# Second-half expert weights requested by the activation engine instead of the sync engine in a two-layer mixture-of-experts kernel

## The reference

```python
# 32 experts; every token goes to 2 of them
h = jax.nn.silu(xi @ w1[e]) * (xi @ w3[e])   # "up": two 1024 x 256 matrices
y = (h @ w2[e]) * rw[:, None]                # "down": one 256 x 1024 matrix
out = zeros.at[row_tok].add(y)
```

## Time and profile before

| what | value |
|---|---|
| median of three runs | 2124.95 us |
| the profiled execution's own time | 2125.96 us |
| its span, first to last instruction | 2124.1 us |
| PE busy | 1958.1 us (92%) |
| ACT busy | 447.0 us (21%) |
| DMA, SP's queue (q1) | 292.55 MB |
| DMA, POOL's queue (q0) | 29.45 MB |
| granted TensorE clock, mean | 0.956 of full speed |

### The profile page before, as it was taken

One profiled execution on the slowest core, in us unless ns is written; L12 is line 12 of the kernel. 1 busy time (PEld: TensorE's weight loads), 2 busy tenths in 40 slices (PEclk: granted clock), 3 DMA queues, 4 the chain that ended last, 5 costly groups with the idle time before them and its releaser, 6 DMA issues. The chain is left out here.

```text
span 2124.1 us, 25898 instructions
## 1 busy us (share of the span) xinstructions
PE 1958.1 (92%) x10102; PEld 1188.8 (56%) x10102; DVE 802.6 (38%) x1957; ACT 447.0 (21%) x1212; POOL 433.2 (20%) x465
## 2 busy tenths in 40 slices
PE   7999897999996999897989993999999989999997
PEld 4566555555553566555445551546579544556973
DVE  1734435211113734436211112145554333455534
ACT  3333211111112333210111110122311112232011
POOL 1101311344331101311333331000330000023100
PEclk9999897999998999897999997999999999999999
DMA  5121066999925121065999953211020021101100
GB/s 212 35 82 40 1 268 241 420 398 365 375 93 215 48 82 41 0 267 193 417 396 381 395 224 114 113 75 70 30 80 1 32 89 68 52 30 70 41 1 40
DMA packets 52824, 323.65 MB, mean 152 GB/s; under 512 B 20876, under 2 KB 22188, under 8 KB 29920
## 3 DMA queue, kind: packets, MB, share of 16 engines
q1 hardware_dynamic: 33344, 292.55, 34.8%
q0 software_dynamic: 19360, 29.45, 3.8%
HBM read 404.47 MB, written 30.93 MB: 205 GB/s over the span
## 5 line engine op out<-in xcount | busy, mean ns | idle before, releaser
L931 PE MATMUL b_bank<-b_arena,b_nat 128*64 128x256 f32 x3008 | 344.3, 382 | 3.6 <-DVE b_nat L1413 2.7
L561 PE MATMUL b_bank<-b_arena 128*128 128x512 f32 (+2 forms) x768 | 308.0, 556 | 2.2 <-issue 2.2
L931 PEld LDWEIGHTS b_bank<-b_arena,b_nat 128*64 128x64 f32 x3008 | 218.9, 138 | 152.6 <-issue 59.7
L1413 DVE TENSOR_TENSOR b_nat<-b_bank,b_prm 128x512 f32<-128x512 f32 x94 | 65.0, 692 | 436.3 <-PE b_bank L913 269.1
L2177 PE MATMUL b_bank<-b_actT,b_ring 128*128 128x512 f32 x512 | 224.0, 594 | 0.0
L561 PEld LDWEIGHTS b_bank<-b_arena 128*128 128x128 f32 x768 | 145.2, 194 | 136.4 <-issue 106.5
L949 PE MATMUL b_bank<-b_arena,b_ebuf 128*64 128x512 f32 x752 | 185.0, 613 | 1.9 <-ACT b_ebuf L1252 1.9
L2163 PE MATMUL b_bank<-b_ring,b_actT 128*128 128x384 f32 (+1 forms) x512 | 174.3, 498 | 5.9 <-DVE b_actT L3025 5.9
L2177 PEld LDWEIGHTS b_bank<-b_actT,b_ring 128*128 128x128 f32 x512 | 96.0, 190 | 114.9 <-issue 113.8
L1385 POOL DMA_INDIRECT y_rows<-b_va,b_rows_ix x94 | 95.5, 1016 | 312.0 <-ACT b_va L1260 302.7
L2163 PEld LDWEIGHTS b_bank<-b_ring,b_actT 128*128 128x128 f32 x512 | 97.6, 194 | 75.2 <-issue 29.7
(11 more groups left out here) (364 smaller groups left out, 2599.6 us busy)
## 6 DMA issues: line engine op xcount, KB each, us to landing
b_arena<-in_w SPq DMA_DIRECT2D x64, 2048.0 KB, 15.0
b_arena<-in_w SPq DMA_DIRECT2D x64, 1024.0 KB, 16.9
b_ring<-in_w_t SPq DMA_DIRECT2D x8, 2048.0 KB, 8.0
b_arena<-in_w SPq DMA_DIRECT2D x8, 1536.0 KB, 10.9
b_ring<-in_w_n2b SPq DMA_DIRECT2D x6, 1536.0 KB, 6.8
b_arena<-in_w_out SPq DMA_DIRECT2D x4, 2048.0 KB, 7.9
b_arena<-y_rows SPq DMA_DIRECT2D x8, 1024.0 KB, 7.9
b_ring<-in_w_out SPq DMA_DIRECT2D x4, 2048.0 KB, 7.8
```

What stands on the lines that cost most here:

```text
L561: ins = pe.matmul(bank[:, 0:width], actT[:, k, tok(i)], w[:, k, :], start=k == 0, stop=k == KD - 1)
L931: ins = pe.matmul(psum[2 + b % 2][f * CAP:(f + 1) * CAP, 0:256], xgT[:, b % 2, k % 4, k // 4, :], w[:, k, f, :], start=k == 0, stop=k == K ...
L1413: return dve.tensor_tensor(out, a, b, op)
```

## The change

SP keeps all up requests, and the down requests of blocks 0 to 5. The down request for block b + 6 is issued by ACT, right behind its copy of the results of block b, for every b whose successor in the slot is an expert block. That is 26 requests in each layer, 52 in all. SP's waits for `moe_y` in that stage are gone. ACT adds no wait: it has waited for `moe_y` of block b ahead of the copy.

```diff
@@ experts(b), on SP
-                    if b >= NSLOT:
-                        sp.wait_ge(sg.sem("moe_y"), NB * l + slot_before(b) + 1)
-                    sp.dma_start(arena[:, mid:end], rows[:, KD * 512:WROW]).then_inc(sg.sem(f"moe_v{slot_of(b)}"), 16)
+                    if b < NSLOT:
+                        sp.dma_start(arena[:, mid:end], rows[:, KD * 512:WROW]).then_inc(
+                            sg.sem(f"moe_v{slot_of(b)}"), 16)
@@ result(b), on ACT
                     act.activation(yo[:, b % 3, :], psum[6 + b % 2][:, :], ACT.Copy).then_inc(sg.sem("moe_y_out"), 1)
+                    if b + NSLOT < NB and BLOCKS[b + NSLOT] < NE:
+                        n = b + NSLOT
+                        e = l * NE + BLOCKS[n]
+                        act.dma_start(arena[:, slot_of(n) * WROW + KD * 512:(slot_of(n) + 1) * WROW],
+                                      A["w123"][e * P:(e + 1) * P, KD * 512:WROW]).then_inc(
+                            sg.sem(f"moe_v{slot_of(n)}"), 16)
```

## The result

The changed kernel takes 2137.2 us (median of five runs, 2133.1 to 2138.74) against 2124.57 us before. The ratio is 1.0058 with a 95% interval of 1.0044 to 1.0073: 12.6 us slower. The profiled execution took 2138.74 us with a span of 2136.9 us, 12.8 us more than the span before.

The account below looks back on a forecast made before the run. PE, busy 92% of the span, was taken to bound the kernel. Layer 0's +4.4 us and layer 1's +0.6 us summed to +5.0 us: 2131.0 us profiled, 2130.0 us median; own range 2127 to 2135 us, wide range 2121 to 2141 us.

Parts of the forecast that it names:

- the list of signs: What would show the forecast right: layer 0 waits 2 to 5 us at L913, its stage takes 4 to 5 us more.
- Where PE waits, and for what: Expert stage: weights come in time; layer 1 waits 11.1 us for gathered tokens of blocks 11 and 14, layer 0 none.
- Earlier up requests, gain 0: SP's waits for down products go; every second up request comes 3 us earlier, nobody waits for it: gain 0.
- ACT's issues, cost 0: 52 down requests on ACT, 0.33 to 1.36 us each, hidden in 3.11 us idle ahead of the hidden copy: 0.
- sign of 0.3 to 0.5 us less idle time ahead of L1252: A sign of the forecast being right: ACT's idle time ahead of L1252 shrinks by 0.3 to 0.5 us.
- A queue of its own for the down matrices: ACT's queue takes turns from POOL's: 4.9 us less 1.7 slack, a 3.2 us wait at layer 0 block 8, +4.4 us.
- The 23.3 us that fitted 23.2: Layer 1, block 11: scatter, overflow load and gather by row turns, 5.5 + 12.3 + 5.5 = 23.3 us; trace 23.2.
- 1.36 us per us of wait: Expert stage: each microsecond PE waits on a gather costs 1.36 us, from 15.1 us more for 11.1 us of waits.
- Layer 1 cancels but for 0.6 us: Layer 1: block 8's new wait and changes at blocks 11 and 14 sum to +0.6 us, bounds -8 and +18.
- much slower: Rival: nothing cancels across the layers' overflow blocks, 2 x 4.4 + 2 x 6.7 = +22 us, 2147 us; chance 0.08.

Follow-up runs that it names:

- late up requests: The changed kernel with SP's old waits for the down products put back, so up requests come at their old times: 2136.96 us, ratio 1.0055 to the kernel before.

## Why the prediction was right, and where its sizes were off

The direction was right, and so were the queue and the wait. The time, 2137.2 us, lies within the wide range, 2121 to 2141 us, but above the forecast's own, 2127 to 2135 us: the loss was 12.6 us where 5.0 had been summed. Layer 0's wait (6.42 us) and its stage (9.1 us more) also lie above what the list of signs allowed.

*Where PE waits, and for what*: right. The weights asked for by SP were in time, the gathers behind the overflow loads were not; without the loads' data both waits are gone.

*Earlier up requests, gain 0*: nearly, for the whole time. With two queues they cost 1.6 us, of uncertain size; with three, the median is the same with and without them (2137.2 and 2136.96 us). Within layer 0 it was wrong. Block 10's request went out at 379.28 us, as worked out, and nobody waits for these weights. But their transfers run beside the overflow load: they added 2.6 us to the wait at block 8 and 3.0 us to the stage, and layer 1 gave 1.4 us back.

*ACT's issues, cost 0*: right, shown with 52 and with 104 of them. The sign of 0.3 to 0.5 us less idle time ahead of L1252 did not show, since the issue is over before the copy is.

*A queue of its own for the down matrices*: the mechanism is shown from three sides. The third queue alone brings the loss (2136.96 us), one queue of either engine does not (2126.68 and 2124.87 us), and the size of the requests that take turns with POOL's moves the time at equal bytes (2106.5 us). For layer 0 its size was nearly right: with late up requests the wait is 3.85 us where 3.2 was summed, and the third queue adds at least 4.0 us to the gather where the sum had 4.9. The stage then loses 6.1 us instead of 4.4. The further 2.6 us of wait in the changed kernel are those of the early requests.

*The 23.3 us that fitted 23.2*: in part luck. In the run with early requests in one queue (another kernel, but with the same two queues) the trace tells when the load itself landed. Overflow load 11 of layer 1 landed 23.4 us after its issue began and PE was released 1.9 us later, in all 25.3 us; the sum had 18.8 us with the issue and then 5.5 us for the gather. At overflow load 8 of layer 0 and load 14 of layer 1 the gather came 1.7 and 1.6 us behind the load. So the gather behind a load was priced too high, and the load or what lies ahead of it too low. That only one scatter lay ahead of it, as the sum has it, no row shows.

*1.36 us per us of wait*: against an undisturbed stage of 278.4 us, a microsecond of wait costs 9.1 / 6.42 = 1.42 us in layer 0 and 20.4 / 14.50 = 1.41 us in layer 1, and 1.58 and 1.37 us in the run with late up requests. It holds, roughly.

*Layer 1 cancels but for 0.6 us*: at blocks 8 to 14 it does. The waits there sum to 11.40 us instead of 11.06, one comes earlier and that of block 14 is gone. What I had not seen is the third wait, 3.10 us at 1212.56 us (block 32), with no real load just in front of it. The engines are full there, 1.01 at 405 GB/s, but full engines and a third queue are not enough for it: without overflow data the changed kernel has a share of 1.02 at 1180 to 1195 us and no wait, and with late up requests the wait is missing too. Its cause is open.

```profile
1200.00:1215.00 15.00, 11.90 (x84) 6.56 (x82) 2.34 (x6) 1.86 (x6) 5.12 (x5) 0.90 1.01 405
```

Layer 1 lost 5.4 us instead of 0.6; with late up requests it lost 6.7 us, and there nothing cancelled: the waits of blocks 11 and 14 sum to 12.04 us instead of 11.06. So the sum was 14.5 in the stages where I had 5.0, and the measured 12.6 lies between my forecast and "much slower", which assumed that nothing cancels.

## What to carry to other kernels

When the DMA engines are full, moving requests to another engine's queue wins no bandwidth and changes who gets it: find out which queue the critical transfers are in before adding a queue beside it. A request that nobody waits for can still take time from one that somebody waits for, by coming earlier or by being large; here up requests cut in two gave 17 us in the kernel before, and cut in four 12 us, since the weights were then late. A wait that is cured by order alone may only move to the next row in the same queue, so look at the waits after the cure.

## What the runs showed of the hardware

SP's requests can take long themselves. Uncut they took at most 1.36 us. Cut in two, one took 1.85 us. Cut in four, one took 9.6 us in the kernel before and 13.4 us in the changed one, while the median was 0.44 and 0.43 us, against 0.33 us uncut. These are SP's requests of the kernel before with quarter rows (ns, min, median, max), and behind them the changed kernel's:

```profile
L511 SPq DMA_DIRECT2D b_arena<-in_w x256: 327/436/9622, 272.4 to 1227.6; - x128
```

```profile
L511 SPq DMA_DIRECT2D b_arena<-in_w x256: 327/434/13438, 274.5 to 1234.2; - x128
```

But they are not what made the weights late. The block that PE waits for until 1073.05 us in the kernel before with quarter rows is block 13. Its four requests went out in order here (start, length of all four):

```profile
1039.90 8.00 SPq L511 DMA_DIRECT2D b_arena<-in_w  x4
```

They were out at 1047.90 us, 25 us before PE had the weights; the long ones at 1049.3 to 1071.1 us, 1.1 to 9.6 us each, are for blocks 15 and 16. In the changed kernel with quarter rows, block 13's four requests took 2.30 us from 1039.40 on, and PE had the weights at 1082.84 us, 41 us later. So it is the data that was late. Whether POOL's larger share alone does that, and what holds SP, was not tested.
